# Dense tiles of a hybrid encoder layer: three chunks of columns, one after another or row by row of the contraction

## What is computed

```python
xn = rmsnorm(x, g_mix)
u_lru, y_lru, q, k, v, gates = jnp.split(xn @ w_in, IN_SPLITS, axis=-1)
xc, lru_conv_new = causal_dwconv(u_lru, lru_conv_prev, w_lconv, b_lconv)
h, lru_h_new = rg_lru(xc, lru_h_prev, w_a, b_a, w_i, b_i, lam)
br_lru = (h * jax.nn.gelu(y_lru)) @ w_br_lru
br_attn = attn_fn(q, k, v, sink) @ w_br_attn
x = x + (g[:, :, 0] * br_lru + g[:, :, 1] * br_attn) @ w_out
gate_pre, up = jnp.split(rmsnorm(x, g_ffn) @ w_up, [D_FF], axis=-1)
gc, ffn_conv_new = causal_dwconv(gate_pre, ffn_conv_prev, w_fconv, b_fconv)
x = x + (jax.nn.gelu(gc) * up) @ w_down
```

## Time and profile before

| what | value |
|---|---|
| median of three runs | 1778.83 us |
| the profiled execution | 1780.82 us |
| its span, first to last instruction | 1778.7 us |
| TensorE (PE) busy | 1770.4 us, 11288 matmuls |
| weight loads (PEld) busy | 1711.9 us, 11288 |
| VectorE (DVE), ScalarE (ACT), POOL busy | 819.7, 572.2, 594.4 us |
| DMA | 90.16 MB, 51 GB/s |
| mean granted TensorE clock | 0.998 |

### The profile page before, as it was taken

The page is one execution under the profiler, slowest core; times in us unless marked ns, Lnnn a source line. Parts: engine busy times, 40 slices in busy tenths (PEclk is TensorE's granted clock), DMA queues, the critical chain, the costliest instruction groups (busy, mean ns, idle before and its releaser), DMA issues.

```text
span 1778.7 us, 30606 instructions
## 1 busy us (share of the span) xinstructions
PE 1770.4 (100%) x11288; PEld 1711.9 (96%) x11288; DVE 819.7 (46%) x1654; ACT 572.2 (32%) x1167; POOL 594.4 (33%) x688
## 2 busy tenths in 40 slices
PE   9999999999999999999999999999999999999999
PEld 8998888899999999999999999999999999999999
DVE  7966667511267774114444555313444411555511
ACT  5546554300187884002222333101333200333300
POOL 2321111233344433334332333333333333333332
PEclk9999999999999999999999999999999999999999
DMA  4011010111111111111311111111111111111113
GB/s 165 25 53 32 25 36 25 36 51 47 39 51 38 53 41 48 47 41 42 146 47 40 44 47 47 48 47 42 41 47 47 48 47 43 39 47 47 47 47 123
DMA packets 33108, 90.16 MB, mean 51 GB/s; under 512 B 7552, under 2 KB 12960, under 8 KB 33056
## 3 DMA queue, kind: packets, MB, share of 16 engines
q1 hardware_dynamic: 29632, 83.32, 14.4%
q10 hardware_dynamic: 3424, 6.11, 1.0%
HBM read 83.70 MB, written 4.73 MB: 50 GB/s over the span
## 4 chain that ended last, share of the span: by engine, by line
PE 97%; DVE 1%; DMA 1%; ACT 0%; POOL 0%; issue 0%; SPq 0%; DVEq 0%
PE banks L478 89%; PE banks L630 2%; PE banks L560 2%; PE banks L593 1%; PE banks L616 1%; PE banks L820 1%; PE banks L570 1%; DVE x_lo L1351 1%; DMA resid<-xT 0%; DVE resid L1344 0%; POOL w_lo L449 0%; DVE merged L1359 0%; DMA w_raw<-W 0%; PE banks L550 0%; PE banks L611 0%
## 5 line engine op out<-in xcount | busy, mean ns | idle before, releaser
L478 PE MATMUL banks<-x_hi,w_hi 128*128 128x352 f32 x1752 | 574.6, 328 | 2.6 <-DVE x_lo L1336 2.5
L478 PE MATMUL banks<-x_hi,w_lo 128*128 128x352 f32 x1752 | 568.1, 324 | 0.0
L478 PE MATMUL banks<-x_lo,w_hi 128*128 128x352 f32 x1752 | 566.3, 323 | 0.0
L445 POOL TENSOR_SCALAR w_hi<-w_raw 128x1024 fp32r<-128x1024 f32 x136 | 149.5, 1099 | 1133.0 <-DMA w_raw<-W 1133.0
L449 POOL TENSOR_TENSOR w_lo<-w_raw,w_hi 128x256 fp32r<-128x256 f32 x544 | 435.4, 832 | 11.3
L478 PE MATMUL banks<-h_hi,w_lo 128*128 128x352 f32 x1152 | 372.7, 323 | 0.0
L478 PE MATMUL banks<-h_hi,w_hi 128*128 128x352 f32 x1152 | 372.4, 323 | 0.0
L478 PE MATMUL banks<-h_lo,w_hi 128*128 128x352 f32 x1152 | 371.6, 323 | 0.0
L478 PEld LDWEIGHTS banks<-x_hi,w_hi 128*128 128x128 f32 x1752 | 330.9, 189 | 14.1 <-issue 11.0
L478 PEld LDWEIGHTS banks<-x_lo,w_hi 128*128 128x128 f32 x1752 | 330.4, 189 | 0.4
L478 PEld LDWEIGHTS banks<-x_hi,w_lo 128*128 128x128 f32 x1752 | 330.0, 188 | 0.0
(11 more groups left out here) (211 smaller groups left out, 1809.5 us busy)
## 6 DMA issues: line engine op xcount, KB each, us to landing
w_raw<-W SPq DMA_DIRECT2D x137, 512.0 KB, 3.4
o_yT<-resid SPq DMA_DIRECT2D x7, 528.0 KB, 4.9
resid<-xT SPq DMA_DIRECT2D x4, 704.0 KB, 10.6
sqsum<-xT ACTq DMA_DIRECT2D x2, 1056.0 KB, 8.3
sqsum<-xT ACTq DMA_DIRECT2D x1, 2112.0 KB, 14.2
resid<-xT SPq DMA_DIRECT2D x4, 352.0 KB, 6.5
w_raw<-W SPq DMA_DIRECT2D x4, 256.0 KB, 5.6
wabs<-wab ACTq DMA_DIRECT2D x8, 128.0 KB, 3.1
```

What stands on the lines that cost most here:

```text
L445: nc.gpsimd.tensor_scalar(w_hi[s][:, :], w_raw[s][:, :], 1.0, 0.0, ALU.mult, ALU.add).then_inc(w_hi_done, 1)
L478: last = nc.tensor.matmul(out[:, 0:cn], w[s if wt is None else wt][:, k * P:(k + 1) * P], x[:, k, cc:cc + cn], start=(k == 0 and j == 0), ...
```

## The change

A second form of a tile, `tile_by_rows`. It waits once for the weights and once for all three banks, and then goes through the rows. In each row, and in each of the three products, the same weights are used for the three chunks in turn, each into its own bank. The three increments come with the last three matmuls. Where a `before` is given it is called for the three chunks together ahead of row 7.

The new form is used in `loop_tiles` (so in the last three pairs of B and of O), in the loop of G0, in all pairs of `up` but the first of the first part, and for the x tile of `down`. The y tile of `down`, the unrolled pairs of B, G0 and O, and everything in R and before stay as they were. No operand, buffer, load or other engine's program is changed.

```diff
+            def tile_by_rows(s, i, p0, hi, lo, free, freed, before=None):
+
+                pe.wait_ge(wx_ready if s == 0 else wy_ready, i + (p0 + 1))
+                pe.wait_ge(free, freed)
+                for k in range(KT):
+                    if before is not None and k == KT - 1:
+                        for n in range(3):
+                            before(n, k)
+                    for j, (w, x) in enumerate(((w_hi, hi), (w_hi, lo), (w_lo, hi))):
+                        for n, (c0, cn) in enumerate(CHUNKS):
+                            last = nc.tensor.matmul(bank[3 * s + n][:, 0:cn], w[s][:, k * P:(k + 1) * P], x[:, k, c0:c0 + cn],
+                                                    start=(k == 0 and j == 0), stop=(k == KT - 1 and j == 2))
+                            if k == KT - 1 and j == 2:
+                                last.then_inc(x_done if s == 0 else y_done, 1)
+
             def loop_tiles(p0, trips, hix, lox, hiy, loy, fx, x0, fy, y0):
                 with pe.Fori(0, trips) as i:
-                    tile(0, i, p0, hix, lox, fx, i * 3 + x0)
-                    tile(1, i, p0, hiy, loy, fy, i * 3 + y0)
+                    tile_by_rows(0, i, p0, hix, lox, fx, i * 3 + x0)
+                    tile_by_rows(1, i, p0, hiy, loy, fy, i * 3 + y0)
...
                 with pe.Fori(0, KT - 3) as i:
-                    tile(0, i, p0 + 2, c_hi, d_lo, x_dve, i * 3 + (xd + 3))
-                    tile(1, i, p0 + 2, x_hi, x_lo, y_act, i * 3 + (ya + 6))
+                    tile_by_rows(0, i, p0 + 2, c_hi, d_lo, x_dve, i * 3 + (xd + 3))
+                    tile_by_rows(1, i, p0 + 2, x_hi, x_lo, y_act, i * 3 + (ya + 6))
...
             def up(f, j, before=None, second=None):
                 pair = f * PAIRS_PER_PART + j
-                tile(0, pair, PAIR_F, h_hi, h_lo, x_dve, f * (UP + DOWN) + j * 3 + X_DVE["F"], before=before)
-                tile(1, pair, PAIR_F, h_hi, h_lo, y_dve, f * (UP + DOWN) + j * 3 + Y_DVE["F"], before=second)
+                xd, yd = f * (UP + DOWN) + j * 3 + X_DVE["F"], f * (UP + DOWN) + j * 3 + Y_DVE["F"]
+                if before is not None:
+                    tile(0, pair, PAIR_F, h_hi, h_lo, x_dve, xd, before=before)
+                    tile(1, pair, PAIR_F, h_hi, h_lo, y_dve, yd, before=second)
+                else:
+                    tile_by_rows(0, pair, PAIR_F, h_hi, h_lo, x_dve, xd)
+                    tile_by_rows(1, pair, PAIR_F, h_hi, h_lo, y_dve, yd)
...
                     pair = f * PAIRS_PER_PART + j
-                    tile(0, pair, PAIR_F + KT, act_hi, act_lo, x_dve, f * (UP + DOWN) + j * 3 + (X_DVE["F"] + UP),
-                         before=last_row(f_lo, f * (3 * KT) + 3 * (KT - 1)))
+                    tile_by_rows(0, pair, PAIR_F + KT, act_hi, act_lo, x_dve, f * (UP + DOWN) + j * 3 + (X_DVE["F"] + UP),
+                                 before=last_row(f_lo, f * (3 * KT) + 3 * (KT - 1)))
                     tile(1, pair, PAIR_F + KT, act_hi, act_lo, y_dve, f * (UP + DOWN) + j * 3 + (Y_DVE["F"] + UP))
```

## The result

The changed kernel takes 1812.69 us, median of four runs (1811.78 to 1813.57), beside 1778.45 for the kernel before (four runs): a ratio of 1.0192, 95% interval 1.0177 to 1.0208, 34 us slower. The forecast was 1783.1, with a range to 1793.

The account below looks back on a forecast made before the run. TensorE's own rate was taken to bound the kernel. Spacing 0, O to F 4.3, other stages 0 and clock 0 gave +4.3 us: 1783.1 us against the median 1778.83, range 1766 to 1793.

Parts of the forecast that it names:

- the point on B and G0: Tile ends in B and G0: readers' 3.5 us are covered by the next tile's 11.6 us, so no wait.
- The passage from O to F: TensorE waits 4.3 us (3.4 to 5.3) for VectorE's nacc, three chains following one another after O's last tile.
- The clock: Behind the wait between O and F: taken as 0, with 2.4 us kept as a possible cost of half clock.
- rival 4: The clock falls in the wait between O and F: 2.4 us more, 1785.5 us; chance 0.07.
- The spacing: Time per matmul inside the 5760 reordered ones stays at 160.9 ns: 0 us, bounds -3 and +7 us.
- Rivals 1, 2 and 3: Reordered matmuls: better operand order, 1763 us (0.20); repeated load isn't paid, 1719 (0.07); every bank change costs, 1806 (0.08).
- B, up, down and the weights: Other stages: readers and weight splits finish in time, 6 us to spare at down, 2.8 us for weights; 0 us.

Follow-up runs that it names:

- e1: Changed kernel with the loop of G0 alone back to chunk after chunk (720 of 5760 matmuls): 1786.81 us, ratio 1.0049.
- e4: Kernel before with the loop of G0 alone by rows: 1804.76 us, ratio 1.0150.
- e8: Changed kernel with O's last pair by chunks, G0's loop by rows with two sets of gate tiles in turn: 1776.11 us, ratio 0.9991.
- e9: Changed kernel with 20 more unused matmuls in each turn of G0's loop before the wait for the y banks: 1803.89 us, ratio 1.0142.
- e2: Changed kernel with only the last y tile of O back to chunk after chunk (72 matmuls): 1806.85 us, ratio 1.0159.
- e3: Changed kernel with both the loop of G0 and the last y tile of O back to chunks: 1783.01 us, ratio 1.0026.
- e10: Changed kernel with 34 more unused matmuls before the wait for nacc between O and F: 1809.66 us, ratio 1.0172.
- e5: Changed kernel with the loop of G0 and the whole last pair of O back to chunks: 1776.75 us, ratio 0.9994.
- e6: Changed kernel with O's last pair by chunks; in G0's loop the x tile by rows, the y tile by chunks: 1783.53 us, ratio 1.0035.
- e7: Changed kernel with O's last pair by chunks; in G0's loop the y tile by rows, the x tile by chunks: 1784.16 us, ratio 1.0040.

## Why the prediction was wrong

- **What failed first** is the point on B and G0: "each reader has one or two operations a chunk", so "3 x 2 x 0.59 = 3.5 us against 11.6: covered". It counted how long the readers work and not when they may begin. In G0 a y bank's reader begins when the next x tile has been joined, because both go through GG. The row said so: ScalarE's gates waited 118.0 us for VectorE's joins, not for TensorE. The cover of a y bank was not the 11.6 us of the x tile but what the x tile's chunks gave each other. Measured: 15.9 us of waits and about 9 us of half clock, 26 in all; e1 and e4 show the place, e8 the cause, e9 the share of the clock.
- **The passage from O to F** was the right mechanism, with its size short. The wait was forecast at 4.3 us (ends 3.4 and 5.3) and measured 5.6, because of the price of a chain: "two chains at 2.31 and one at 3.25" were 2.5, 3.6 and 2.8, 9.0 us together: two of the three ran beside POOL's split (964.3 to 968.7), and the forecast took one. VectorE's timeline in the changed kernel (three residuals, and the last nacc):

```profile
960.49 0.53 DVE L1695 TENSOR_TENSOR resid<-banks,sqsum 128x352 f32 x1 [2.42 <-PE banks L504]
...
963.01 0.52 DVE L1695 TENSOR_TENSOR resid<-banks,sqsum 128x352 f32 x1
...
966.63 0.51 DVE L1695 TENSOR_TENSOR resid<-banks,sqsum 128x352 f32 x1
...
968.96 0.51 DVE L1702 TENSOR_TENSOR nacc<-nacc,ntmp 128x352 f32<-128x352 f32 x1
```

  In the changed kernel the x tile ahead added nothing to this, since VectorE had been idle for 2.42 us when y's first chain began. Its lateness counts once y goes by chunks (e2, e3).
- **The clock** was rival 4, with a chance of 0.07 and 2.4 us for one place. In the changed kernel it came behind all six waits: 4.5 us behind O, 9 in G0. "I take nothing" set aside the one row that it had, the wait of 2.1 us with half clock behind it, because it lay at the start. In e2 a wait of 2.2 us in the middle of full-clock work had half clock behind it as well, though the small matmuls may have a part in that (e10). The rule of the Trainium skill that the prediction names (page "TensorE: Matmul & The Clock Gate", HAM oscillation), that TensorE left idle goes back to half clock, was the better guide, and e9 agrees in G0: with work in the wait there is no half clock.
- **The spacing** was forecast unchanged, and is: 160.8 ns in F, 160.5 in G0 (e8), 1776.75 us for e5. Rivals 1, 2 and 3, together 0.35 of the chances, are out. Each matmul has its load as before, and a bank change on every matmul costs nothing that shows in the spacing.
- **B, up, down and the weights** were covered, as worked out: TensorE has no wait there in the changed kernel.

## What to carry to other kernels

When a tile's results come all at its end instead of in turn, ask of every bank not how long its readers work but what its reader waits for. A buffer with one set behind the bank ties it to the other slot's tile, and then the pipelining by chunks was the cover. In G0 the waits of 3.2 us cost in the mean half as much again through the clock (9 us on 15.9), so five short waits were dearer than the one that I looked for. An order that leaves loads and matmuls as they are gives nothing to pay for such waits.

## What was not expected of the hardware

The changed kernel, e2, e4 and e10 have the five waits of 3.2 us in G0, 20 in all, each in the middle of full-clock work. Over the 7 us behind them the granted clock is 0.76 to 0.79 in 14 cases, 0.55 to 0.59 in five, and 1.00 in one, e4's first. Shorter waits in the passage from O to F had half clock behind them too, 2.9 us (e3) and 2.2 us (e2); there the small matmuls come next, and e10 leaves their part open. The ten of 1.1 to 1.3 us in e6 and e7 had none. So the length of a wait alone doesn't tell what the clock will cost; what else decides it stays open. The stretch behind the 2.2 us of e2:

```profile
968.40:972.00 3.60, 3.60 (x13) 3.60 (x14) 2.74 (x14) 0.27 (x1) 0.00 (x0) 0.50 0.02 5
```

The kernel before at its start, at half clock (start us, us of one matmul):

```profile
10.43 0.49 PE L478 MATMUL banks<-x_hi,w_lo 128*128 128x352 f32 x1
10.73 0.49 PE L478 MATMUL banks<-x_hi,w_hi 128*128 128x352 f32 x1
11.02 0.49 PE L478 MATMUL banks<-x_lo,w_hi 128*128 128x352 f32 x1
```

There the starts are 0.29 to 0.30 us apart, which is 352 columns at 1.2 GHz (293 ns) and nothing more. Only at full clock is there an excess, 14 ns over 146.7, and the two orders differ in it by 0.6 ns at most (72 matmuls of `down` take 11.56 us by chunks and 11.60 by rows, e5).
